# Decode attention: latent keys turned in 32x32 blocks by VectorE, scores on sixteen TensorE tiles, one stage and one ring of buffers for modulation and decode

## What is computed

```
mod = silu(c) @ w_ada + b_ada            # c: 8 samples and the prompt, w_ada 1024 x 6144 (24 MB)
q_lat = einsum(q_nope, w_uk)             # 8 heads x 256 per sequence
s_past = q_lat . lat_past + q_rope . kr_past      # lat_past 8 x 8192 x 256, kr_past 8 x 8192 x 32
p = softmax([s_past, s_new])
o_lat = p . [lat_past, latent]
```

## Time and profile before

| | us |
|---|---|
| median of three runs | 2026.57 |
| the profiled execution's own time | 2019.72 |
| its span | 2017.9 |
| its first stage and decode stage (start to the next stage's first load) | 404.1 |

### The profile page before, as it was taken

How to read it: one execution, slowest core, us unless ns; L and a number is a source line. 1 busy time by engine, 2 the same in 40 slices (tenths; PEclk the granted TensorE clock), 3 DMA queues, 4 the chain that set the end, 5 groups by cost and what they waited for, 6 DMA issues and landing times. The chain is left out here.

```text
span 2017.9 us, 31568 instructions
## 1 busy us (share of the span) xinstructions
PE 1763.9 (87%) x12773; PEld 1574.5 (78%) x12773; DVE 862.7 (43%) x1657; ACT 562.5 (28%) x1025; POOL 201.3 (10%) x174
## 2 busy tenths in 40 slices
PE   5889999849799788988879829999999999999981
PEld 2467777629799666666759829999999999999981
DVE  1234444473343544454532863433343334333437
ACT  1134444342211243534443332111211111111123
POOL 1032222020000202020202320000000000000006
PEclk8899999959899878878789959999999999999995
DMA  9697767150111100000023222111211121212013
GB/s 362 235 395 262 275 258 266 51 162 19 51 43 42 32 0 14 1 13 0 0 78 100 75 81 67 50 45 31 62 37 57 31 62 31 62 31 62 1 49 140
DMA packets 116489, 183.39 MB, mean 91 GB/s; under 512 B 17038, under 2 KB 86358, under 8 KB 112300
## 3 DMA queue, kind: packets, MB, share of 16 engines
q1 hardware_dynamic: 106428, 101.71, 16.0%
q0 software_dynamic: 8192, 75.85, 9.9%
q10 hardware_dynamic: 1776, 4.51, 0.6%
HBM read 172.06 MB, written 9.94 MB: 90 GB/s over the span
## 5 line engine op out<-in xcount | busy, mean ns | idle before, releaser
L1951 PE MATMUL ps<-mix_conv,wf_hl 128*128 128x384 f32 (+1 forms) x1584 | 272.4, 321 | 11.3 <-DVE wf_hl L1976 11.3
L1951 PE MATMUL ps<-mix_attn,wf_hl 128*128 128x384 f32 (+1 forms) x1584 | 271.0, 319 | 0.0
L1951 PEld LDWEIGHTS ps<-mix_conv,wf_hl 128*128 128x128 f32 x1584 | 255.1, 189 | 11.4 <-DVE wf_hl L1976 11.4
L1951 PEld LDWEIGHTS ps<-mix_attn,wf_hl 128*128 128x128 f32 x1584 | 253.7, 188 | 0.0
L1965 PE MATMUL ps<-hid,wd_hl 128*128 128x384 f32 (+1 forms) x1584 | 249.9, 318 | 0.0
L1965 PEld LDWEIGHTS ps<-hid,wd_hl 128*128 128x128 f32 x1584 | 248.8, 188 | 0.0
L1991 DVE TENSOR_TENSOR h<-ps,gate 128x384 f32<-128x384 f32 (+1 forms) x66 | 34.0, 516 | 320.3 <-PE ps L1951 320.3
L2006 DVE TENSOR_TENSOR acc<-ps,acc 128x384 f32<-128x384 f32 (+1 forms) x240 | 123.8, 516 | 93.4 <-PE ps L1965 93.4
L1022 PE MATMUL ps<-U,wc_hl 128*128 128x384 f32 (+1 forms) x864 | 138.3, 323 | 8.7 <-DVE wc_hl L1036 8.7
L1022 PEld LDWEIGHTS ps<-U,wc_hl 128*128 128x128 f32 x864 | 138.1, 191 | 9.0 <-DVE wc_hl L1036 9.0
L473 PE MATMUL ps<-ident,lat_raw 128*128 128x128 f32 x1024 | 125.7, 276 | 12.0 <-DMA lat_raw<-in_cache_latent,idx 11.5
(11 more groups left out here) (313 smaller groups left out, 2497.1 us busy)
## 6 DMA issues: line engine op xcount, KB each, us to landing
w_ada_sb<-in_w_ada SPq DMA_DIRECT2D x12, 2048.0 KB, 19.6
wf_raw<-in_w_gate SPq DMA_DIRECT2D x22, 512.0 KB, 4.0
wf_raw<-in_w_up SPq DMA_DIRECT2D x22, 512.0 KB, 5.3
wd_raw<-in_w_down SPq DMA_DIRECT2D x22, 512.0 KB, 5.8
wc_raw<-in_w_in SPq DMA_DIRECT2D x24, 256.0 KB, 3.1
x_nat<-in_x_prompt SPq DMA_DIRECT2D x4, 1024.0 KB, 8.3
wo_raw<-in_w_o SPq DMA_DIRECT2D x8, 512.0 KB, 4.0
ln_x<-in_x_prompt SPq DMA_DIRECT2D x8, 512.0 KB, 4.4
```

Source lines behind the costliest of these rows:

```text
L1951: last = pe.matmul(ps[:, 2 * (q % 2) + g, 0:tn], a, x, start=j == 0, stop=j == 3 * KD - 1)
```

## The change

The two stages become one, `phase_sample`, with one barrier at its end.

- `w_ada` chunks and gathered latent rows share one ring of six 16 KB-a-partition buffers. SyncE may load a chunk when the one six earlier has been read. GpSimd gathers group g (g < 6) when chunk 6+g has been read (at that time its buffer is free), later ones when group g-6 has been weighed.
- The interleaved projections move one chunk forward (after chunks 4, 5, 6, 7 and 8). After chunk 9 TensorE does four new 128-column matmuls which bring `q_lat` into blocks of 32 rows, and VectorE copies them to `q32` (128 x 8 x 8 x 32).
- TensorE no longer turns rows. VectorE turns them in 32x32 blocks, SBUF to SBUF: per group four instructions of 128x1024 and one of 128x512 for the rotated key. The PSUM copies at 537, 558 and 575 are gone.
- Scores are matmuls of 32 rows x 32 columns x 128 streamed columns on the sixteen 32x32 tiles of the array: per group 8 x 16 for the latent and 16 for the rotated key, 144 calls. The four row tiles write four PSUM banks.
- The copy of the turned probabilities moves from VectorE to ScalarE. The PSUM banks of the scores are no longer doubled, so the scores of group g wait for the exponential of g-1.

VectorE's slot t is now: turns of group t (two), maximum and negative of t-1, turns of t (two more and the key), merges. TensorE's slot: scores of t-1, weighing of t-2, turned probabilities of t-1.

```diff
+                for g in range(NGR):
+                    if g < RING:
+                        pool.wait_ge(ada_sum, ADA - RING + g + 1)
+                    else:
+                        pool.wait_ge(weighed, g - RING + 1)
+                    pool.indirect_dma_start(ring[:, (ADA + g) % RING], None, lat_rows_d, ...
...
+                    if n == 9:
+                        pe.wait_ge(dve1, V["q_lat"])
+                        for b in range(4):
+                            last = pe.matmul(ps[:, 7, b * P:(b + 1) * P],
+                                             q_pick[:, b, :], q_lat[:],
+                                             start=True, stop=True)
...
+                def score(g):
+                    s = g // GPS
+                    pe.wait_ge(turned, g + 1)
+                    wait(pe, exp_out, g)
+                    for b in range(8):
+                        for a in range(4):
+                            rows = slice(32 * a, 32 * a + 32)
+                            for c in range(4):
+                                pe.matmul(ps[32 * c:32 * c + 32, a, 0:P], q32[rows, s, b, :],
+                                          latT[rows, g % 2, 4 * c:4 * c + 4, b, :], start=b == 0, stop=False)
+                    for a in range(4):
+                        rows = slice(32 * a, 32 * a + 32)
+                        for c in range(4):
+                            last = pe.matmul(ps[32 * c:32 * c + 32, a, 0:P], zk[rows, s, :],
+                                             krT[rows, g % 2, 4 * c:4 * c + 4, :], start=False, stop=True)
+                    last.then_inc(scored, 1)
...
+                for t in range(NGR + 2):
+                    if 0 <= t - 1 < NGR:
+                        score(t - 1)
+                    if 0 <= t - 2:
+                        weigh(t - 2)
+                    if 0 <= t - 1 < NGR:
+                        turn_p(t - 1)
...
+                def turn_rows(g, c):
+                    at = slice(4 * c, 4 * c + 4)
+                    dve.transpose(latT[:, g % 2, at].rearrange("p i b n -> p (i b n)"),
+                                  rows_of(g)[:, at].rearrange("p i d -> p (i d)"))
...
                 for t in range(SLOTS):
                     if t < NGR:
+                        dve.wait_ge(lat_in[t % RING], 16 * (t // RING + 1))
+                        wait(dve, scored, t - 1)
+                        turn_rows(t, 0)
+                        turn_rows(t, 1)
...
+                        turn_rows(t, 2)
+                        turn_rows(t, 3)
+                        dve.wait_ge(kraw_in[t % RING], 16 * (t // RING + 1))
+                        dve.transpose(krT[:, t % 2].rearrange("p i n -> p (i n)"),
+                                      kraw[:, t % RING].rearrange("p i d -> p (i d)")).then_inc(turned, 1)
```

More of the change, by code:

```diff
@@ L167, in _ @@
                 for n in range(12):
-                    wait(sp, ada_sum, n - ADA_BUF + 1)
-                    sp.dma_start(w_ada_sb[:, n % ADA_BUF], w_ada[:, :, n * 512:(n + 1) * 512]).then_inc(ada_in[n % ADA_BUF], 16)
+                    wait(sp, ada_sum, n - RING + 1)
+                    sp.dma_start(chunk(n), w_ada[:, :, n * 512:(n + 1) * 512]).then_inc(ada_in[n % RING], 16)
                 sp.wait_ge(dve1, V["kr"])
@@ L174, in _ @@
                 sp.wait_ge(out1, 32)
+                for seq in range(NS):
+                    sp.wait_ge(merged, seq + 1)
+                    for j in range(PARTS):
+                        sp.dma_start(io["o_scratch"][seq, j], o_row[32 * j:32 * j + H, seq % 2, :]).then_inc(o_free[seq % 2], 16)
+                sp.wait_ge(o_free[0], 64 * (NS // 2 + 1))
+                sp.wait_ge(o_free[1], 64 * (NS // 2 + 1))
             @block.gpsimd
@@ L237, in modulate @@
                         at = 32 * (k % 4)
-                        last = pe.matmul(ps[at:at + 32, 1 + n % 2, :], cT[:, k, :], w_ada_sb[:, n % ADA_BUF, k, :],
+                        last = pe.matmul(ps[at:at + 32, 1 + n % 2, :], cT[:, k, :], chunk(n)[:, k, :],
                                          start=k < 4, stop=k >= 4)
@@ L282, in _ @@
                         for k in range(KV):
[L283 removed]
+                            last = pe.matmul(ps[0:NS, 3, :], new_latT[:, k, :], w_uk[:, k, :], start=k == 0, stop=k == KV - 1)
                         last.then_inc(pe1, 1)
[L285 removed]
+                    if n == 7:
                         pe.wait_ge(dve1, V["q"])
@@ new lines, in turn_p, with weigh @@
+                def turn_p(g):
+                    pe.wait_ge(exp_out, g + 1)
+                    wait(pe, pT_out, g)
+                    for i in range(4):
+                        last = pe.transpose(ps[:, PTURN, i * P:(i + 1) * P], p_sb[:, i].rearrange("p a n -> p (a n)"), ident[:])
+                    last.then_inc(p_turned, 1)
+                def weigh(g):
+                    pe.wait_ge(pT_out, g + 1)
+                    wait(pe, o_out, g)
+                    for i in range(4):
+                        for c in range(4):
+                            last = pe.matmul(ps[32 * c:32 * c + 32, PO, 0:KVR], pT[:, g % 2, i, c, :],
+                                             rows_of(g)[:, 4 * c + i, :], start=i == 0, stop=i == 3)
+                    last.then_inc(weighed, 1)
@@ L301, in _ @@
                 order = Order(dve, dve1_order)
+                dve.memset(pT[:], 0.0).then_inc(pT_clear, 1)
+                for b in range(2):
+                    dve.memset(o_row[:, b], 0.0).then_inc(o_free[b], 64)
                 for z in (q32, zk):
@@ L387, in _ @@
                 for r in range(4):
-                    order.mark(dve.tensor_copy(zk[32 * r:32 * r + 32, :, r, 0:H], src))
+                    order.mark(dve.tensor_copy(zk[32 * r:32 * r + 32, :, 0:H], src))
+                mod(7)
+                dve.wait_ge(pe1, E["q_lat"])
+                dve.tensor_copy(q_lat[:], ps[:, 6, 0:P]).then_inc(dve1, 1)
+                mod(8)
+                dve.wait_ge(pe1, E["q_blocks"])
+                for k in range(KV):
+                    src = ps[:, 7, :].rearrange("p (b k h s) -> p k s b h", b=4, k=KV, h=H)[:, k]
+                    order.mark(dve.tensor_copy(q32[:, :, 4 * k:4 * k + 4, 0:H], src))
+                order.wait()
                 dve.wait_ge(pe1, E["k_new"])
@@ L392, in _ @@
                 order.then(dve.tensor_copy(kn[:, :, NOPE:], kr_s[:].unsqueeze(1).to_broadcast([NS, H, ROPE])))
[L393 to L401, removed]
+                order.then(dve.tensor_tensor(prod, q[:], kn, ALU.mult))
+                order.mark(dve.tensor_reduce(s_new[:], prod, AX_X, ALU.add))
                 for n in range(9, 12):
```

344 lines of the change are left out of this document (127 added, 217 removed).

## The result

The changed kernel takes 2156.09 us (median of four, 2140.43 to 2162.12) against 2026.12: ratio 1.0637, 95% interval 1.0582 to 1.0693. It is slower by 6%; forecast were 1967 us and a range of 1930 to 2050. The profiled execution took 2140.43 us (span 2138.6), so it stands to 2019.72 of before, 120.7 us apart. The next stage's first load moved from 404.06 to 526.61, by 122.5 us: all of the loss lies in the window that the change rewrote.

What follows compares the result with a forecast made beforehand. TensorE was taken to bound the decode stage (40.00 of 40.00 us busy). The window was 92 + 32 x 7.7 + 13.1 = 351.5 us against 404.1, 52.6 less, so 2019.7 became 1967 us; range 1930 to 2050.

Steps and rivals of the forecast that it cites:

- Instruction supply: Decode stage: 324 pairs a group need 2.7 fetches, 2.5 us of one DMA engine; at worst 8.6 us a group, at best nothing added.
- Rival C: Decode stage: TensorE fed or clocked too slowly, 8.8 us a group or fetches adding up to 8.6; 2002 us, chance 0.15.
- The scores: TensorE's decode slot: 288 matmuls with weight loads on sixteen tiles at once, 1.96 us a group, plus 0.2 to land.
- the burst of four loads: Trace row behind the scores' price: four weight loads last 0.13 us where one lasts 0.11, so starts at most 7 ns apart.
- Rival A: Decode scores: tiles issued one by one, pairs 27.2 ns apart, TensorE the bound at 10.4 us a group; 2054 us, chance 0.22.
- VectorE's slot: Decode stage: turns, maximum, negative and merges run in order, 6.67 us a slot, the least period.
- Equal within 0.1: Decode stage: scores of 1.96 + 0.2 us against VectorE's two turns of 2.28; only 0.1 put on the path.
- The clock: Decode stage: at TensorE's low clock scores 3.9, weighing 3.7, probabilities 0.9, changes 0.3: 8.8 us a group; part of a 0.15 chance.
- The start: Before the decode stage: first turn at 92 us, between 89 and 97, with barrier, memsets and first gather's latency off the path.
- So moving work ahead pays: First stage: TensorE's last modulation chunk starts at 89.67 though landed at 80.5, so earlier projections help bring the first turn to 92.
- The end: After the last turn: scores through merge 9.7 us, then 3.4 to the next stage, together 13.1 us.
- 32 x 7.7: Decode stage: 32 groups at a period of 7.7 us, from 6.67 + 0.1 and 0.9 for supply and low clock, against 8.97.

Runs made afterwards that it cites:

- the loop with the maximum last: Changed kernel with TensorE's decode stage as a hardware loop, weighing only groups 0 and 1's rows, and VectorE's maximum behind all turns of the slot: 1976.88 us.
- the loop with the original order: Changed kernel with TensorE's decode stage as a hardware loop over pairs of groups, weighing only groups 0 and 1's rows, VectorE's order kept: 2044.02 us.
- the join alone: Kernel before with only the joined stage, one ring, early gathers and steps one chunk earlier; TensorE still turns rows and scores on four column tiles: ratio 0.9993.

## Why the prediction was wrong

**The step that failed** is "Instruction supply". It saw the right resource and counted 2.7 fetches of 16 KB a group; but it priced a fetch by its packet, 0.94 us of one DMA engine, and put the worst case at 6.1 + 2.5 = 8.6 us. A fetch's price is not its share of the DMA but its round, 3.45 us with the engines free and 5.2 behind gathers, and no second one is under way meanwhile: 2.53 x 5.2 = 13.2 us. (A fetch holds 256 instructions, so a group's 648 are 2.53; the 2.7 came from taking 31 fetches in 32 groups.) The earlier trace rows could not show it, since the kernel before used one fetch in 9.3 us and hid the whole round. Rival C named the mechanism ("by gaps inside a group's scores next to an instruction fetch") and stopped at "no gain left near 9.3": right in kind, too small by 3.5 us a group. It had a chance of 0.15 and nearly all of it on the faster side.

**The scores** at 6.8 ns a pair, from the burst of four loads, were wrong too. In the loop with the maximum last, where nothing interrupts them, pairs start every 12.8 ns (median over 60 pairs at the full clock), and a group takes 4.0 us from the first start to the last end, where the forecast had 1.96 + 0.2. Rival A's 27.2 ns were as wrong on the other side. The Trainium skill, "TensorE: Matmul & The Clock Gate", Wait — 56ns, not 53.3ns?, which the prediction weighed, gives about 25 ns as the least distance of matmuls; here the traces disagree: 128 matmuls on changing 32x32 tiles take 1.89 us, of which the last's own length is about 0.27, so (1.89 - 0.27) / 127 = 12.8 ns.

**VectorE's slot** was right. One turn measured 1.215 us and four in a row 4.62, where 4.56 was taken; the period with the supply out of the way and the maximum last is 6.93 us where the sum had 6.67 + 0.1. But the sum held only for that order. With the maximum in the middle the slot is scores plus what follows, and the loop with the original order ran at 9.31. The prediction checked the scores against two turns by its 1.96 us ("Equal within 0.1"); at 4.0 us the check fails by itself. So even with most of the fetches gone the change as written gave 2044 us in its one execution, about 1% slower than the kernel before beside it (2025.42).

**The clock** was placed as a rival cause of its own (C, 8.8 us). In these runs it follows TensorE's idle time, whatever makes it idle: 0.78 to 0.83 with the gaps of the fetches, 0.86 to 0.88 in the loop that waits for turns, 0.98 to 1.00 in the loop with the maximum last. It adds to the loss (the weighing's matmul 573 ns against 382) and goes with its cause.

**The start**: 92 forecast, 104.07 measured. "So moving work ahead pays" failed: TensorE's chain of small steps and chunks runs almost without a pause from 62 us on, so an earlier place for some steps only puts off others. The early gathers also took from `w_ada`: its last chunk had been expected at 80.5 and was still awaited at 96.95 in the join alone, and at 110.59 in the execution without gathers and with the maximum last. The end was 526.6 - 507.4 (end of the last turn) = 19.2 us, not 13.1: TensorE began the last scores 2.0 us after the last turn, since it had to finish a weighing and turned probabilities first, and they took 6.3 us, not 2.2, with one more stall of 1.6 in them.

The difference adds up: from the first turn to the end of the last it took 507.4 - 104.07 = 403.3 us, not 32 x 7.7 = 246.4, which is 156.9 more; the start is 12.1 and the end 6.1 more, together 175.1, and the window missed its forecast by 526.6 - 351.5 = 175.1.

## What to carry to other kernels

Count instructions as well as columns. Straight-line code on TensorE that runs through 256 instructions (128 matmuls with their loads) in less than 3.5 us outran its own supply here, and under the gathers it got 256 in 5.2 us in the mean. The profile puts the gaps down to "issue"; their sign is a q8 packet that starts some 2.4 us before the gap ends. The way out is fewer and longer instructions, or a hardware loop of fixed addresses whose body stays resident (some 1,300 instructions did). And a cut of one engine's work by small tiles must be summed again for the order of the others: the place of one maximum was worth next to nothing here at first and 67 us once the supply no longer bound.

And look at all executions, not only at the profiled one: the window of the join alone was 6 us shorter in its profile (398.50 against 404.06), and over twelve executions there was no gain at all.

## What the runs showed of the hardware

- TensorE's instructions come 256 at a time (16 KB packets; the changed kernel has 51 more of them than the kernel before, for 32 x 408 more instructions, 256 each). In straight-line code no fetch started less than 3.3 us behind the one before: 2.4 us go from the fetch's start to the next matmul, though the packet itself takes about 0.95. The Trainium skill, "Runtime: NRT & Kernel Launch", Instruction fetch mechanics, has the same blocks of 16 KiB and calls crossing one "mostly hidden", because the engine issues more slowly than the fetch fills. The trace agrees on the block (119 packets, 1.95 MB) and disagrees on the rest: 128 pairs ran in 1.89 us and 5.13 us of nothing followed.
- Instruction packets wait behind the gathers' packets that are already queued: 98.1% of the engines' time went to rows in the 3 us before the fetch at 327.45, and wherever a fetch started over 2 us after a gap's end in the changed kernel, rows took 84 to 99% of the time between.
- A loop body of some 1,300 instructions goes round without fetches (no packet of q8 from 160 to 340 us). The same section of the Trainium skill gives TensorE's store as 128 KiB, 2048 instructions, which would hold it; no run here shows where the limit lies.
- VectorE's turn of 128x1024 float32 in 32x32 blocks takes as long as a copy of that size: 1.215 us against 1.224 for the copy from PSUM that it replaces.
- Matmuls that go round the sixteen 32x32 tiles (128 columns, float32, full clock) start 12.8 ns apart in the median over 60, with either order of the tiles.
